# A ConvFFN down projection from seven half products, and tail norms from one product with a matrix of ones

## The chip, the cores and the metric

One NeuronCore of a Trainium2 chip runs the kernel. The metric is the device time of one execution in microseconds, as the median of the timed runs. Everything is in f32.

## The reference, cut to what matters

Two layers over 1088 tokens (1024 of a prompt, 64 of eight sampled sequences), model width 1024, hidden width 2816. Each layer mixes the tokens (a recurrence in the first, attention in the second), then runs a convolutional feed-forward net. What follows the mixer is here called the tail of a layer:

```python
x = x + rmsnorm(mo, g[1])            # mo: the mixer's output after its last matrix
hn = rmsnorm(x, g[2])
fo, cs = conv_ffn(hn, conv0[layer], ...)
x = x + rmsnorm(fo, g[3])            # layer 0: rmsnorm(x, ...) of the next layer follows

def rmsnorm(x, g):
    y = xf * lax.rsqrt(jnp.mean(xf * xf, axis=-1, keepdims=True) + NORM_EPS)
    return y * g
def conv_ffn(xn, prev, wup, cw, cb, wdown):
    hid = xn @ wup                   # 1024 -> 2 * 2816
    ...                              # a convolution of three taps along the tokens
    gate, val = jnp.split(c, 2, axis=-1)
    out = (jax.nn.gelu(gate, approximate=True) * val) @ wdown   # 2816 -> 1024
```

## The kernel before

Activations lie transposed, 128 channels on the partitions and all 1088 tokens along the free axis. `m.X`, `m.H`, `m.big` (22 tiles of 1088), `m.w`, `m.tmp` and `m.lanes` are regions of SBUF that every stage cuts up anew. Each engine has its own program, written out by hand in the order in which it runs; semaphores (`wait_ge`, `then_inc`) tie them together, and nothing reorders them. Within a tail (function `tail`, called once per layer) PE runs four stages.

1. The mixer's last matrix (`mixer`, L241): 3 token blocks of 384, 384 and 320 columns (`TB`) by 8 output tiles. A block and an output tile are a unit; its sum over the contraction tiles goes to one of six PSUM banks.
2. The up projection. For f = 0, 1 and 21 the products are plain (`expand`, L269). For f = 2 to 20 (`SEVEN`) the two output tiles, two halves of the contraction and two halves of the tokens are multiplied by seven products instead of eight (`seven`, L299): sums of quarter matrices of weights are built by Pool (`weight_sums`, L622 to L633), sums of quarters of tokens once by DVE (`token_sums`, L534 to L539), and DVE and ACT combine the products. DVE then convolves (L569, L573), ACT takes the gelu (L415), DVE multiplies with the other half (`gated`, L579) into `hid`, tile f of `m.big`.
3. The down projection (L338): again 24 units, each a sum over 22 tiles of `hid`. The weights of an output tile (1408 KB) alternate between two buffers, `wdt[0]` and `wdt[1]`, and are loaded anew for each of the three token blocks.
4. The norms, of the mixer's output with residual and following norm (p = 0), and of the down projection's output (p = 1; in the second layer without a following norm).

A norm runs block by block beside the next block's units. ACT copies the unit out of PSUM (L381) and squares it (L370), DVE adds the squares of the eight output tiles (L471). PE multiplies the sum with one column of ones, so that the tokens' sums of squares come to stand on the partitions (`statistic`, L221). ACT takes the root of three columns (L374), DVE the reciprocal of three columns (L475). PE spreads them over all partitions by a product with the identity (`spreading`, L229). DVE scales by it (L485), Pool adds the residual in `m.X` (L650), ACT squares again, and for the second norm the same follows up to L497.

The numbers count(p, n, b) say which norm of which block a semaphore has reached. SP issues all loads and stores in one queue. In the recurrence's stage (`rwkv_core`) it loads weights, a table `pv` of vectors per channel, the first key tile and eight more constants; PE, ACT and DVE each wait there for all nine loads of the semaphore `consts`. PE then builds masks with the constants (L1827, L1829) and only then computes the gates of the first pair of heads (`gates`, L1691), which ACT takes (L1337) and which DVE's scan (L1440) needs.

## Time and profile before

| | us |
|---|---|
| median of three timed runs | 4157.53 |
| lowest, highest | 4154.57, 4160.07 |
| the profiled execution, its own time | 4153.73 |
| its span | 4151.9 |

| stage of the profiled execution | from | to |
|---|---|---|
| recurrence (`rwkv_core`), first load | 402.1 | |
| first tail: mixer's last matrix | 1130.5 | 1257.8 |
| up projection | 1257.8 | 1839.7 |
| down projection | 1839.7 | 2167.2 |
| end of its norms, first load of attention | | 2189.3 |
| second tail: mixer's last matrix | 3147.2 | 3228.2 |
| up projection | 3228.2 | 3810.1 |
| down projection | 3810.1 | 4134.8 |
| end of its norms and of the last store | | 4151.9 |

Times are read from one profiled execution, in us from the start of its span; 1.8 us lie around the span. An f32 product appears as two records of PE. Records of PE's weight loads (PEld) run beside the products. A row of the timeline gives start, duration, engine, line, operation, what is written and read, and in brackets how long the engine had been idle before and who released it.

### The profile page before, as it was taken

The numbers are of one execution on the slowest core, as the hardware profiler recorded it, in microseconds if no ns is written. First come the engines' busy times: TensorE is split into PE (matmuls) and PEld (weight loads), VectorE is DVE, ScalarE is ACT, GpSimd is POOL, SyncE is SP. The second block draws the span as 40 slices with busy tenths as digits, with TensorE's granted clock in tenths as the row PEclk, the third lists the DMA queues.
The fourth block names the chain that finished last, engine by engine and source line by source line (L and its number), as shares of the span: only waits on it lengthen the run. The fifth ranks groups of instructions, "written<-read, shape, count | busy, mean of one in ns | idle before, by whom it ended". The sixth has DMA issues, their size and how long they took to land. (4 is left out here: it accounts for less than half of the span.)

```text
span 4151.9 us, 79805 instructions
## 1 busy us (share of the span) xinstructions
PE 3773.5 (91%) x35200; PEld 2817.8 (68%) x35200; DVE 1996.3 (48%) x3258; ACT 815.7 (20%) x1859; POOL 516.6 (12%) x432
## 2 busy tenths in 40 slices
PE   7998687888699999999988999999648999999998
PEld 4887566666466888865666777777535688886566
DVE  8441676666435666640124464746613566664001
ACT  6110344333121110010011222222212100001000
POOL 1221000000011222200011010101001122220001
PEclk9999899999899999999998999999768999999999
DMA  2222011010111111123321111111183111112223
GB/s 78 84 84 94 30 36 38 28 35 27 66 74 40 46 43 42 43 96 109 115 99 69 55 38 45 51 40 46 55 334 113 56 43 42 43 43 98 110 98 127
DMA packets 97216, 291.80 MB, mean 70 GB/s; under 512 B 37224, under 2 KB 52968, under 8 KB 88040
## 3 DMA queue, kind: packets, MB, share of 16 engines
q1 hardware_dynamic: 96872, 286.70, 19.5%
q8 instruction: 279, 4.57, 0.5%
q14 instruction: 65, 0.53, 0.0%
HBM read 237.71 MB, written 48.95 MB: 69 GB/s over the span
## 5 line engine op out<-in xcount | busy, mean ns | idle before, releaser
L338 PE MATMUL ps<-sb_big,sb_w 128*128 128x384 f32 (+1 forms) x2112 | 646.6, 468 | 1.2 <-ACT sb_tmp L428 1.2
L338 PEld LDWEIGHTS ps<-sb_big,sb_w 128*128 128x128 f32 x2112 | 400.2, 190 | 241.6 <-ACT sb_tmp L428 2.2
L299 PE MATMUL ps<-sb_h,sb_w 128*128 128x272 f32 x1672 | 408.1, 392 | 1.4 <-ACT sb_tmp L428 1.4
L299 PEld LDWEIGHTS ps<-sb_h,sb_w 128*128 128x128 f32 x1672 | 317.5, 190 | 67.7 <-issue 2.3
L299 PE MATMUL ps<-sb_x,sb_w 128*128 128x272 f32 x1216 | 291.1, 392 | 0.0
L471 DVE TENSOR_TENSOR sb_tmp<-sb_tmp 128x384 f32<-128x384 f32 (+1 forms) x63 | 34.8, 552 | 526.7 <-ACT sb_tmp L370 525.0
L299 PEld LDWEIGHTS ps<-sb_x,sb_w 128*128 128x128 f32 x1216 | 231.0, 190 | 47.6
L573 DVE SCALAR_TENSOR_TENSOR sb_big<-sb_tmp,sb_big 128x1024 f32<-128x1024 f32 (+1 forms) x176 | 204.0, 1159 | 13.4 <-issue 0.3
L2080 PE MATMUL ps<-sb_h,sb_w 128*128 128x384 f32 (+1 forms) x576 | 186.9, 468 | 0.0
L1099 PE MATMUL ps<-sb_x,sb_w 128*128 128x272 f32 x768 | 183.8, 392 | 0.0
L269 PE MATMUL ps<-sb_h,sb_w 128*128 128x384 f32 (+1 forms) x576 | 178.6, 470 | 3.9 <-DVE sb_tmp L548 2.1
L1099 PEld LDWEIGHTS ps<-sb_x,sb_w 128*128 128x128 f32 x768 | 145.9, 190 | 30.1
L381 ACT ACTIVATE sb_h<-ps 128x384 f32<-128x384 f32 (+1 forms) x72 | 34.0, 473 | 642.1 <-PE ps L338 598.2
L269 PEld LDWEIGHTS ps<-sb_h,sb_w 128*128 128x128 f32 x576 | 108.4, 190 | 69.3 <-issue 5.6
L2236 ACT ACTIVATE sb_w<-sb_w,sb_tmp 128x128 f32<-128x128 f32 (+1 forms) x192 | 84.9, 443 | 335.4 <-DVE sb_tmp L2341 335.4
L573 DVE SCALAR_TENSOR_TENSOR sb_w<-sb_tmp,sb_w 128x1024 f32<-128x1024 f32 (+1 forms) x176 | 142.5, 810 | 13.5 <-issue 0.4
L299 PE MATMUL ps<-sb_x,sb_lanes 128*128 128x272 f32 x608 | 145.5, 392 | 0.0
L299 PE MATMUL ps<-sb_x,sb_tmp 128*128 128x272 f32 x608 | 145.5, 392 | 0.0
L2101 PE MATMUL ps<-sb_x,sb_w 128*128 128x272 f32 x576 | 145.0, 398 | 0.0
L1773 PE MATMUL ps<-sb_tmp,sb_big 64*64 64x64 f32 x4352 | 103.0, 226 | 45.2 <-DVE sb_w L1563 32.7
L2296 DVE TENSOR_TENSOR sb_big<-sb_big,ps 128x272 f32<-128x272 f32 x120 | 52.6, 438 | 190.1 <-PE ps L2101 187.1
L1099 PE MATMUL ps<-sb_big,sb_w 128*128 128x272 f32 x576 | 140.3, 393 | 3.1 <-DVE sb_big L977 2.6
(345 smaller groups left out, 6128.0 us busy)
## 6 DMA issues: line engine op xcount, KB each, us to landing
sb_w<-wdown SPq DMA_DIRECT2D x46, 1408.0 KB, 6.0
sb_w<-wup SPq DMA_DIRECT2D x88, 512.0 KB, 4.3
sb_w<-wqkv SPq DMA_DIRECT2D x36, 512.0 KB, 3.8
sb_big<-kT SPq DMA_DIRECT2D x8, 2304.0 KB, 14.6
sb_big<-vc SPq DMA_DIRECT2D x8, 2304.0 KB, 16.3
sb_w<-wrkv SPq DMA_DIRECT2D x24, 512.0 KB, 5.4
rkv_scratch<-sb_big SPq DMA_DIRECT2D x18, 544.0 KB, 6.3
sb_big<-rkv_scratch SPq DMA_DIRECT2D x16, 544.0 KB, 3.6
```

The lines of the kernel that those rows point to most:

```text
L269: mm = pe.matmul(m.ps[:, 3 * q + b, 0:n], wt[f % 2][q][:, k, :], m.H[:, k, t0:t0 + n], start=(k == 0), stop=(k == KT - 1))
L299: mm = pe.matmul(m.ps[:, 2 * HOME[f][p] + e, 0:PIECE], w, rhs[:, k, e * PIECE:(e + 1) * PIECE], start=(k == 0 and p not in ("P2", "P3")), ...
L338: mm = pe.matmul(m.ps[:, u % 6, 0:n], wdt[u % 2][:, f, :], hid[:, f, t0:t0 + n], start=(f == 0), stop=(f == FT - 1))
L381: act.activation(out[:, k, t0:t0 + n], m.ps[:, u % 6, 0:n], ACT.Copy)
L471: dve.tensor_tensor(acc, acc, SQ[p][n][:, slot(n, b, k), 0:w], ALU.add).then_inc(summed[n], 1)
L573: ins = dve.scalar_tensor_tensor(out=out, in0=tap(j), scalar=cw(j), in1=out, op0=ALU.mult, op1=ALU.add)
L1099: mm = pe.matmul(m.ps[:, bank, 0:PIECE], lhs[:, k, :], rhs(k), start=(k == 0 and p not in ("P2", "P3")), stop=(k == 3), skip_group_check=True)
L1773: mm = pe.matmul(m.ps[o, bank, col0:col0 + C], lhs[r, c, :], rhs[r, c, :] if len(rhs.shape) == 3 else rhs[r], start=(q == 0), stop=(q == l ...
L2080: mm = pe.matmul(m.ps[:, ring(s, p), 0:w], wt[t][:, k, :], m.H[:, k, t0:t0 + w], start=(k == 0), stop=(k == KT - 1))
L2101: mm = pe.matmul(m.ps[:, ring(s, p), 0:PIECE], lhs[:, k, :], rhs[:, k, :], start=(k == 0 and n not in ("P2", "P3")), stop=(k == 3), skip_g ...
L2236: ins = act.activation(SM[n % 2][:, h, lo:2 * P], SM[n % 2][:, h, lo:2 * P], ACT.Exp, bias=nm[:, n, h:h + 1], accum_out=zz[:, n, h:h + 1])
L2296: dve.tensor_tensor(out, kept, ps, op).then_inc(ptd, 1)
```

## The change

- **Down projection.** It runs in eight pairs n of output tiles: `u = n // 4` chooses half of the tokens (544 columns, two quarters of 272), `n % 4` the pair of output tiles. The contraction is cut in two halves of 11 tiles (`HF`). Of each pair come seven products (`DOWN`, in the order P1, P7, P2, P6, P5, P4, P3), each over 11 tiles and 272 columns; P2 adds to the bank of P1 and P3 to that of P5. The four quarter matrices of weights of a pair, W11, W21, W12 and W22 (704 KB each), have one buffer each. Pool builds W3 = W11 - W21, W2 = W22 - W3, W21 = W21 + W22 and W2 = W12 - W2. DVE builds four sums of the hidden quarters (`hidden_sum`) for each half of the tokens, those of the first half for 10 of 11 rows between f = 20 and f = 21. ACT copies the products P1 and P2 out, DVE combines the other five (`combine`), and ACT squares the results.
- **Norms.** The statistic is one product of a matrix of ones with the sum of squares, so that every partition has every token's sum. ACT's root and DVE's reciprocal work on all columns (384, 320 or 272), and there is no spread. In the down projection the blocks are four quarters of 272 tokens. Blocks 0 and 1 run beside pairs 4 and 5, blocks 2 and 3 after pair 7; the second norm of these two is summed by PE, eight products each (`late_statistic`).
- **Residual.** It is loaded in two halves into other places (`XIN`) instead of in one piece into `m.X`; the results are stored in quarters.
- **Recurrence.** `pv` signals with the weights, PE computes the first gates before it waits for the constants, and DVE normalizes the first key before it waits for them.

```diff
+    HF = FT // 2
+    DOWN = ("P1", "P7", "P2", "P6", "P5", "P4", "P3")
+    BY_DVE = ("P6", "P7", "P5", "P4", "P3")
...
@@ sync
+            def part_in(n, q, r, dst, signal):
+                sp.dma_start(dst, a["wdown"][layer, 2 * (n % 4) + q, :, r * HF:(r + 1) * HF, :]).then_inc(signal, 16)
...
-            for u in range(2, NU):
-                sp.wait_ge(product, NU + u - 1)
-                sp.dma_start(wdt[u % 2], a["wdown"][layer, u % KT]).then_inc(wd[u % 2], 16)
...
+            for n in range(1, NDOWN):
+                sp.wait_ge(product, down(n - 1, "P7"))
+                part_in(n, 0, 0, W11, a11_in)
...
+                sp.wait_ge(product, down(n - 1, "P5"))
+                part_in(n, 1, 0, W21, a21_in)
+                sp.wait_ge(sums_done, WSUMS + 4 * n)
+                part_in(n, 0, 1, W12, a12_in)
+                sp.wait_ge(product, down(n - 1, "P4"))
+                part_in(n, 1, 1, W22, a22_in)
@@ tensor
-            def statistic(p, n, b):
-                pe.wait_ge(summed[n], NSUM * p + (KT - 1) * (b + 1))
-                acc = ACC[p][n][:, b % 2 if n == 0 else 0, :]
-                for j, (t0, w) in enumerate(subs(b)):
-                    mm = pe.matmul(m.ps[0:w, 6, j:j + 1], acc[:, t0:t0 + w], m.ones[:, 0:1], start=True, stop=True)
-                mm.then_inc(stat, 1)
...
+            def statistic(n, b):
+                pe.wait_ge(summed[n], (KT - 1) * (b + 1))
+                w = TB[b][1]
+                pe.matmul(m.ps[:, 6, 0:w], m.ones[:, :], ACC[n][:, b % 2 if n == 0 else 0, 0:w], start=True,
+                          stop=True).then_inc(stat, 1)
...
-                    for f in range(FT):
...
-                        mm = pe.matmul(m.ps[:, u % 6, 0:n], wdt[u % 2][:, f, :], hid[:, f, t0:t0 + n], start=(f == 0), stop=(f == FT - 1))
...
+            def seventh(n, p):
+                u = n // 4
+                lhs, rhs = {"P1": (W11, lambda k: half(u, 0, 0)[:, k, :]), "P7": (W3, lambda k: tsum(3, k, k + 1)[:, 0, :]),
+                            "P2": (W12, lambda k: half(u, 1, 0)[:, k, :]), "P6": (W2, lambda k: tsum(2, k, k + 1)[:, 0, :]),
+                            "P5": (W21, lambda k: half(u, 0, 1)[:, k, :]), "P4": (W22, lambda k: tsum(4, k, k + 1)[:, 0, :]),
+                            "P3": (W2, lambda k: half(u, 1, 1)[:, k, :])}[p]
...
+                for k in range(HF):
+                    if (n, p, k) == (0, "P7", HF - 1):
+                        pe.wait_ge(hidden, FT + 1)
+                    mm = pe.matmul(m.ps[:, BANK[n, p], 0:PIECE], lhs[:, k, :], rhs(k), start=(k == 0 and p not in ("P2", "P3")),
+                                   stop=(k == HF - 1), skip_group_check=True)
...
@@ vector
+                if f == FT - 2:
+                    for j in (3, 1, 2, 4):
+                        hidden_sum(j, 0, 0, HF - 1)
+            for j in (3, 1, 2):
+                hidden_sum(j, 0, HF - 1, HF)
+            hidden_sum(4, 0, HF - 1, HF).then_inc(hidden, 1)
...
+            def block_invert(n, b):
+                dve.wait_ge(rooted, stat_at(n, b))
+                dve.reciprocal(DROOT[b % 2], DROOT[b % 2])
...
+            block_residual(2, meanwhile=lambda: block_invert(0, 3))
+            block_residual(3)
+            dve.drain()
+            for k in range(4):
+                dve.tensor_tensor(XS[1][:, k, :], XIN[3][:, k, :], TMP2[1][:, k, :], ALU.add).then_inc(conv, 1)
+            if two_norms:
+                block_invert(1, 2)
+                block_normed(2)
+                block_invert(1, 3)
+                block_normed(3)
@@ gpsimd
+            for n in range(NDOWN):
+                pool.wait_ge(a11_in, 16 * (n + 1))
+                pool.wait_ge(a21_in, 16 * (n + 1))
...
+                pool.tensor_tensor(W3, W11, W21, ALU.subtract).then_inc(sums_done, 1)
+                pool.wait_ge(a22_in, 16 * (n + 1))
...
+                pool.tensor_tensor(W2, W22, W3, ALU.subtract).then_inc(sums_done, 1)
+                pool.tensor_tensor(W21, W21, W22, ALU.add).then_inc(sums_done, 1)
...
+                pool.wait_ge(product, down(n, "P6"))
...
+                pool.tensor_tensor(W2, W12, W2, ALU.subtract).then_inc(sums_done, 1)
@@ rwkv_core
-            sp.dma_start(pv, a["pv"].rearrange("i p n -> p i n")).then_inc(consts, 16)
+            sp.dma_start(pv, a["pv"].rearrange("i p n -> p i n")).then_inc(ld_w, 16)
...
-            pe.wait_ge(consts, 9 * 16)
+            for g in range(3):
+                gates(0, g)
+            pe.wait_ge(consts, 8 * 16)
```

The order of PE at the start of the first layer's down projection. Before, nine units of 22 products run without a break, then come the first statistic (L221) and its spread (L229):

```order
L269 MATMUL ps<-sb_h,sb_w 128x384 x16
L269 MATMUL ps<-sb_h,sb_w 128x320 x8
L338 MATMUL ps<-sb_big,sb_w 128x384 x198
L221 MATMUL ps<-sb_ones,sb_tmp 128x1 x3
L338 MATMUL ps<-sb_big,sb_w 128x384 x22
L229 MATMUL ps<-sb_ident,sb_small 128x128 x3
```

In the changed kernel (whose lines are numbered anew; L424 is `seventh`) the products of pair 0 stand there, P1, P7, P2, P6, P5, P4 (in two regions) and P3, the last one together with P1 of pair 1:

```order
L424 MATMUL ps<-sb_big,sb_w 128x272 x11
L424 MATMUL ps<-sb_x,sb_tmp 128x272 x11
L424 MATMUL ps<-sb_big,sb_w 128x272 x11
L424 MATMUL ps<-sb_x,sb_w 128x272 x11
L424 MATMUL ps<-sb_big,sb_tmp 128x272 x11
L424 MATMUL ps<-sb_x,sb_w 128x272 x10
L424 MATMUL ps<-sb_lanes,sb_w 128x272
L424 MATMUL ps<-sb_big,sb_w 128x272 x22
```

Each product needs another weight matrix, three of them made by Pool or shared with its sums. Pool had only the residual's additions there, long after the last weight sums of the up projection (L622 to L633):

```order
L632 TENSOR_TENSOR sb_w<-sb_w,sb_lanes 128x384 [waits t0_up]
L633 TENSOR_TENSOR sb_tmp<-sb_w,sb_lanes 128x128
L650 TENSOR_TENSOR sb_x<-sb_x,sb_tmp 128x384 [waits t0_scaled,x_moved]
L650 TENSOR_TENSOR sb_x<-sb_x,sb_tmp 128x384 [waits t0_scaled] x6
L650 TENSOR_TENSOR sb_x<-sb_x,sb_tmp 128x384 [waits t0_applied]
```

Now it makes four sums of 1408 columns per pair, of which each waits for a load or for a product that last read the buffer (pairs 0 and 1):

```order
L931 TENSOR_TENSOR sb_tmp<-sb_w,sb_tmp 128x1408 [waits t0_conv,t0_a21_in,t0_a11_in]
L938 TENSOR_TENSOR sb_w<-sb_w,sb_tmp 128x1408 [waits t0_hidden,t0_a22_in]
L939 TENSOR_TENSOR sb_tmp<-sb_tmp,sb_w 128x1408
L949 TENSOR_TENSOR sb_w<-sb_w 128x1408 [waits t0_product,t0_a12_in]
L931 TENSOR_TENSOR sb_tmp<-sb_w,sb_tmp 128x1408 [waits t0_product,t0_a21_in,t0_a11_in]
L938 TENSOR_TENSOR sb_w<-sb_w,sb_tmp 128x1408 [waits t0_product,t0_a22_in]
```

In pairs 4 and 5 eight residual additions stand between L939 and L949. On DVE the sums of the hidden halves (L732 to L738) have come in between the gating of f = 20 (L725) and the convolution of f = 21:

```order
L725 TENSOR_TENSOR sb_big<-sb_big,sb_w 128x1088 [waits t0_conv,t0_gelu]
L732 TENSOR_TENSOR sb_x<-sb_big 128x2720 [waits t0_hidden]
L734 TENSOR_TENSOR sb_big<-sb_big 128x10x272
L737 TENSOR_TENSOR sb_x<-sb_big 128x2720
L738 TENSOR_TENSOR sb_x<-sb_x,sb_big 128x2720
L709 COPY sb_tmp<-sb_tmp 128x2 [waits t0_padded,t0_rows_out1,t0_vec1]
```

Before, the convolution followed the gating directly.

## Rows read from the trace of the kernel before

**Rows 1.** Page: busy us (share) xinstructions; a line group, busy and mean ns.

```profile
PE 3773.5 (91%) x35200; PEld 2817.8 (68%) x35200; DVE 1996.3 (48%) x3258; ACT 815.7 (20%) x1859; POOL 516.6 (12%) x432
...
L2296 DVE TENSOR_TENSOR sb_big<-sb_big,ps 128x272 f32<-128x272 f32 x120 | 52.6, 438 | 190.1 <-PE ps L2101 187.1
```

**Rows 2.** Chain of waits, second tail: start, us, what.

```profile
3291.07 487.92 PE ps L299 x2128
...
3810.09 127.98 PE ps L338 x396
3938.07 0.56 PE ps L221 x6
...
3952.93 0.67 PE ps L229 x6
...
4134.84 0.02 issue
```

**Rows 3.** Busy us by window, engines PE, PEld, DVE, ACT, POOL; granted clock.

```profile
1321.00:1809.00 488.00, 487.60 (x2128) 403.94 (x2126) 296.66 (x494) 48.73 (x95) 111.99 (x92) 1.00 0.13 43
1840.00:2167.00 327.00, 327.00 (x1104) 205.63 (x1103) 42.12 (x77) 29.67 (x68) 15.35 (x16) 1.00 0.34 125
3147.00:3228.00 81.00, 71.20 (x240) 44.86 (x240) 37.57 (x67) 29.57 (x69) 16.59 (x16) 0.91 0.23 85
```

**Rows 4.** Timeline, first tail, last up products and start of the down projection.

```profile
1819.01 1.29 DVE L579 TENSOR_TENSOR sb_big<-sb_big,sb_w 128x1088 f32<-128x1088 f32 x1
...
1825.16 0.17 DVE L563 COPY sb_tmp<-sb_tmp 128x2 f32<-128x2 f32 x1 [4.86 <-ACT sb_tmp L428]
...
1839.71 30.58 PE L338 MATMUL ps<-sb_big,sb_w 128*128 128x384 f32 x94 [0.59 <-ACT sb_tmp L428]
...
1844.42 1.29 DVE L579 TENSOR_TENSOR sb_big<-sb_big,sb_w 128x1088 f32<-128x1088 f32 x1
```

**Rows 5.** Lines: xcount, ns min/median/max, first and last start, forms.

```profile
L622 POOL TENSOR_TENSOR sb_tmp<-sb_w x38: 1265/1267/1957, 1315.2 to 3738.8; 128x512 f32<-128x512 f32 x38
...
L2064 POOL TENSOR_TENSOR sb_w<-sb_w x12: 1254/1266/2307, 2196.9 to 2867.2; 128x512 f32<-128x512 f32 x12
...
L534 DVE TENSOR_TENSOR sb_x<-sb_h x2: 2424/2424/2425, 1296.2 to 3266.5; 128x2176 f32<-128x2176 f32 x2
...
L1542 DVE RECIPROCAL sb_lanes<-sb_lanes x8: 1845/1846/1853, 561.7 to 1117.3; 128x272 f32<-128x272 f32 x8
```

**Rows 6.** Loads: xcount, KB each, median us from issue to landing.

```profile
sb_w<-wdown SPq DMA_DIRECT2D x46, 1408.0 KB, 6.0
sb_w<-wup SPq DMA_DIRECT2D x88, 512.0 KB, 4.3
```

**Rows 7.** Timeline of PE, second tail's mixer stage.

```profile
3190.83 0.83 PE L221 MATMUL ps<-sb_ones,sb_big 128*128 128x1 f32 x6 [3.35 <-DVE sb_big L471]
3191.52 4.24 PE L241 MATMUL ps<-sb_big 128*128 128x384 f32 x8
...
3219.31 1.44 PE L221 MATMUL ps<-sb_ones,sb_big 128*128 128x1 f32 x6 [4.71 <-DVE sb_big L471]
```

**Rows 8.** Timeline, end of the first tail.

```profile
2167.16 0.44 ACT L381 ACTIVATE sb_h<-ps 128x320 f32<-128x320 f32 x1 [11.75 <-PE ps L338]
...
2185.26 3.76 DVE L497 SCALAR_TENSOR_TENSOR sb_h<-sb_x,sb_gains,ps 128x320 f32<-128x320 f32 x8 [1.93 <-PE ps L229]
2189.29 1.28 SPq L2032 DMA_DIRECT2D sb_w<-wqkv  x3
```

**Rows 9.** Timeline, end of the second tail.

```profile
4139.64 6.57 POOL L650 TENSOR_TENSOR sb_x<-sb_x,sb_tmp 128x320 f32<-128x320 f32 x8 [66.87 <-DVE sb_tmp L485]
```

**Rows 10.** Timeline, start of the recurrence.

```profile
411.50 1.55 PE L1827 MATMUL ps<-sb_tmp 64*64 64x64 f32 x24 [14.46 <-DMA sb_tmp<-c_level]
...
413.56 3.90 PE L1691 MATMUL ps<-sb_big,sb_tmp 64*64 64x384 f32 x24
...
418.51 2.42 DVE L1440 TENSOR_TENSOR_SCAN sb_big<-sb_tmp,sb_big 128x1088 f32<-128x1088 f32 x1 [3.29 <-ACT sb_big L1337]
```

More of the change, by code:

```diff
@@ L143, in tail @@
-        norms = [2, 2 if g_next is not None else 1]
-        subs = lambda b: [(j * P, min(P, TB[b][1] - j * P)) for j in range((TB[b][1] + P - 1) // P)]
-        def count(p, n, b):
-            return 2 * NBLK * p + norms[p] * b + n + 1
+        ACC = (tiles(m.big, 17 * T + 3 * BW, 2, BW), tiles(m.big, 17 * T + 7 * BW, 1, BW))
+        SQ = (tiles(m.big, 17 * T, 3, BW), tiles(m.big, 17 * T + 5 * BW, 2, BW))
+        TMP = tiles(m.big, 17 * T + 8 * BW, 3, BW)
+        W11, W12, W22, W2 = (tiles(m.w, j * HF * P, HF, P) for j in range(4))
@@ L401, in _ @@
-            collect(0)
-            root(0, 0, 2)
+                    act.wait_ge(added, KT * b + k + 1)
+                    square(1, b, k, m.X[:, k, t0:t0 + n]).then_inc(squared, 1)
+            for b in range(NBLK):
+                for k in range(KT):
+                    take(b, k)
+                    if b and k == 0:
+                        root(0, b - 1)
+                    if b and k == 2:
+                        squares(b - 1)
+                    if b and k == 5:
+                        root(1, b - 1)
@@ L404, in _ @@
+            root(0, 2)
             for s in range(4):
@@ L479, in residual @@
+            def residual(b):
                 t0, w = TB[b]
-                dve.wait_ge(spread, count(p, 0, b))
+                dve.drain()
                 for k in range(KT):
@@ L654, in rwkv_inputs @@
+            pool.wait_ge(m.x_moved, stored + 32)
+            for b in (2, 3):
+                for k in range(KT if b == 2 else 4):
+                    k += 0 if b == 2 else 4
+                    block_scaled(b, k)
+                    pool.tensor_tensor(XS[b - 2][:, k, :], XIN[b][:, k, :], TMP2[b - 2][:, k, :], ALU.add).then_inc(added, 1)
 def rwkv_inputs(m, a, scratch):
@@ L1830, in _ @@
             mm.then_inc(small_ps, 1)
-            for g in range(3):
-                gates(0, g)
             key_sums(0)
```

560 lines of the change are left out of this document (385 added, 175 removed).

## The prediction

> **What bounds the kernel now.** I read the page's busy shares first: PE works 91% of the span and no other engine more than half [rows 1]. A share is only an average, so next comes the chain of waits, stage by stage. From 3291 us on, the chain of the second layer's tail is almost nothing but PE: 487.9 us of up products, then the down stage from 3810.09 to 4134.84, broken only by the small norm products of L221 and L229 [rows 2]. The reader should see that no DMA and no other engine stands between them. The windows say the same of the first layer: in 1840 to 2167 PE is busy for 327.0 of 327.0 us at granted clock 1.00, DVE for 42, ACT for 30, Pool for 15 [rows 3]. So in the down stage columns fewer on PE are time off the end, as long as weights, sums and evictions keep up. In the second layer's mixer window (3147 to 3228) it is otherwise: the clock is 0.91 and PE waits 3.35 us and 4.71 us for DVE's additions [rows 3, 7]. There a gain on PE alone brings nothing.
>
> **The change part by part.**
>
> **Down stream, second layer.** Before: 4134.84 - 3810.09 = 324.75 us [rows 2]. After: 8 pairs of output tiles, 7 products each, 11 contraction tiles, and each f32 product stands as two PE records: 8 x 7 x 11 x 2 = 1232 records of 272 columns. The up stage has just this shape, with fewer factors per product: 487.92 us for 2128 records, 0.2293 us each [rows 2]. 1232 x 0.2293 = 282.5 us, one product 5.04 us, one pair ("cycle") 35.3 us. Three statistics stand in the stream (blocks 0, 1 and 2), two records of 272 columns each: 3 x 0.46 = 1.4. Together 283.9, a change of **-40.9**.
>
> **Down stream, first layer.** Before: from 1839.71 [rows 4] to the last eviction at 2167.16 [rows 8], 327.4 us. After: 282.5 + five statistics (2.3) = 284.8. A change of **-42.6**.
>
> Those two terms hold only with cover, so here is one cycle, counted from the start of P1: P7 ends at 10.1, P2 at 15.1, P6 at 20.2, P5 at 25.2, P4 at 30.2, P3 at 35.3.
> - Pool's sums. A sum of 512 columns takes 1.27 us, up to 2.31 when it meets other work [rows 5]. For 1408 columns that is 3.5 to 6.3 us, four per cycle 14 to 25 of 35.3 us. The tightest is W3 of the next pair: W21 is asked for at 25.2 when P5 is done. 704 KB lies between loads of 4.3 us (512 KB) and 6.0 us (1408 KB) [rows 6], so it lands at about 30 and W3 is ready at 33.5 to 37.5. P7 wants it at 40.3. W2 starts when P3 ends and is ready 3.5 to 6.3 later for P6 at 50.4, W21+W22 by 42 to 48 for P5 at 55.4, the last one starts at 20.2 for P3 at 30.2. None is late; the least slack is 2.8 us. In pairs 4 and 5 Pool has eight residual additions of under 1 us between its third and fourth sum; it starts them at 7 to 13 and is through by 20 or so. I take no stall.
> - SP issues four weight loads per cycle; behind its waits for products only the next weight loads and the residual's transfers are queued, and W11, W12 and W22 have over 10 us of slack.
> - DVE combines five products (an addition of a PSUM tile of 272 columns takes 0.44 us [rows 1]) and adds squares. In pair 3 four sums of the hidden halves come on top. The same kind of subtraction takes 2.42 us for 2176 columns [rows 5], so 3.3 for 2992: 13.3 us in a cycle where it else has little to do. Six PSUM banks let PE run about five products ahead. In pairs 4 and 5 DVE's norm work ends near 24, and the statistic that waits for it stands at 25.2: 1 to 2 us of slack, the second tightest place.
>
> **Start of the down stage.** P7 of pair 0 needs the hidden sums. 40 of 44 rows are added after the tile f=20 is gated (L579 at 1819.01 plus 1.3): four instructions of 2720 columns at 3.0, 12.1 us, until 1832.4. DVE was idle 4.86 us before 1825.16 and then until 1839.7; the convolution of f=21's first half moves to about 1837 [rows 4]. W3 is then ready at 1841 to 1843.5, while P1 keeps PE until 1844.75. The last tile is gated at 1845.7 and four small sums end at about 1847.6; P7 reaches that tile at 1849.3. All hidden, cost 0; if the sums took twice as long, the second convolution would be late and up to 10 us would show in each layer.
>
> **Norms of the mixers.** From L221 to L229 14.86 us pass, where a unit alone takes 127.98 / 9 = 14.22: 0.64 for a statistic, and 0.67 for a spread, 1.31 us for the two [rows 2]. One product with ones of 384 columns costs 0.65, of 320 columns 0.54. First layer, all PE-bound: 4 x 0.66 + 2 x 0.77 = **-4.1**. On DVE the reciprocal grows: 1.85 us for 272 columns [rows 5], so 2.6 for 384, where before it worked on three columns. In the first layer this replaces the wait of one PE unit for the spread. In the second layer DVE's chain bounds: the residual steps start about as before (reciprocal against spread), so I count 0 in the stream (between -2.5 and +3) and **-1.5** for the two norms that fall into the first up products.
>
> **Tail of each layer.** Before, second layer: 17.1 us from 4134.84 to the end of the span. After, from the end of P3: combine, square, add 1.5; eight scalings in 0.42 to 0.47 steps (3.76 us for eight of 320 columns [rows 8]) with a reciprocal of 1.85 in the middle until 6.9; eight more until 10.3; four additions on DVE until 11.8; the last quarter's store about 5. That is 17: **0** (-1 to +2). The old chain had Pool in step with DVE, 6.57 us of additions from 4139.64 [rows 9]; the new one has more on DVE and less handshake. First layer: 22.1 us from 2167.16 to the next stage's first load at 2189.29 [rows 8]. After: squares of the last block by 14.3, sums on PE 15, and on DVE reciprocal, 3.4, reciprocal, 3.4: 22.7. **+0.6** (-1 to +4).
>
> **Start of the recurrence.** PE waited until 411.50 for the last constants, ran the masks and only then the gates at 413.56; ACT took them and DVE's scan began at 418.51 [rows 10]. With the gates ahead of the constants they run from about 405, the masks at 411.5 stay, and the scan can begin at about 414.5, after the masks: **-4.0** (-1.5 to -5). Everything behind it hangs on this chain.
>
> **Sum.** -40.9 - 42.6 - 4.1 - 1.5 + 0 + 0.6 - 4.0 = -92.5. On the profiled execution's own 4153.73 us: 4061.2. The median of the three runs is 3.8 above it, so as a median 4157.53 - 92.5 = **4065**.
>
> **A rule weighed against a row.** Pool's sum of L2064 takes 1.27 us in the median and 2.31 at worst, while DVE subtracts SBUF tiles beside it [rows 5]. The Trainium skill (SBUF - State Buffer, Who interferes with whom) says that a DVE instruction with two SBUF inputs and a GpSimd instruction that reads SBUF exclude each other for their whole length. By the rule every such meeting costs the later one the rest of the earlier; the trace agrees with it in that row. It would put each sum near the upper figure in pair 3 and change nothing elsewhere, since the combines of the steady cycle read PSUM.
>
> **The rivals.**
> - *Supply.* The W3 sum misses P7. For: it is the tightest handover, its load is issued 15 us before it is wanted, W12's load follows it closely, and a 1408-column sum was never seen. Against: with both upper prices 2.8 us remain. If load and sum together took 17 us instead of 15.1, 2 us would be lost in 14 handovers: +28, **4093**.
> - *Ends.* The work without cover costs more: reciprocals and DVE additions against Pool's at the two ends, hidden sums at the two starts, DVE in the second mixer. 3 us in each of four places: +12, **4077**. For: most rows there are scaled from other widths. Against: none is far.
> - *Slower than before: the clock.* In the second mixer PE waits 3.35 us, and the eight records after it take 4.24 us [rows 7], where 8 x 0.323 = 2.6 is full pace [rows 2]: 1.6 more; after the last such wait the small statistic takes 1.44 instead of 0.83. If P7 waited so in each cycle, the low level (1.2 GHz) would cost as much again as the time spent at it. To be slower than before, 92.5 us must be lost in 14 handovers, 6.6 us each: a wait of 5 us and 1.6 for the clock. It decides when load and sum take 20 us instead of 9. The result, with 7 us each, is 14 x 7 = +98, **4163 or more**. Against: the up stage cycles banks in the same way at granted 1.00 [rows 3]. The Trainium skill (TensorE: Matmul & The Clock Gate, A second HAM failure mode: psum-queue depth-cycling) tells of a kernel whose clock swung because PE cycled PSUM banks with short gaps; rows 3 speak against it here.
> - *The norms and the recurrence bring nothing* (the part that would not do what it says): 4.1 + 1.5 + 4.0, **4075**. For: PE's own saving is worth something only where PE bounds, and in the second mixer it does not; at the recurrence DVE might wait for the masks rather than for the gates. Against: in the first mixer PE is the bound, and the gates of rows 10 stand plainly between masks and scan.
>
> **How the numbers follow.** Forecast within about 8 us of 4065: 0.66. Ends or norms, 4073 to 4082: 0.18. Supply, 4080 to 4100: 0.10. More gain than forecast (DVE's chain in the second mixer shortened by 2.5, more at the recurrence), down to 4052: 0.03. Slower: 0.02. The rest is no change: 0.01. The range that leaves out no more than two in ten goes from 4050 to 4086. What a measurement here can tell from no change is about 0.2%, 8 us. Faster by more: 0.97; within: 0.01; slower: 0.02.
>
> **What would show it.** Right: each down stage one PE block of about 284 us at clock 1.00, with no wait of P7 or of the statistic of pair 4; product after product every 5.04 us; the scan of the recurrence at about 414.5; DVE's reciprocals of 2.6 us. Wrong: Pool's 1408-column sums above 6.3 us, idle time of PE before P7 released by Pool, a granted clock under 1.00 inside the stage, or more than 19 us after the last product.

## The result, and the profile after

The changed kernel takes 4101.25 us (median of four runs, 4098.92 to 4110.88) beside 4156.05 for the kernel before in the same comparison: a ratio of 0.9872, 95% interval 0.9853 to 0.9892. A second comparison gave 4105.65 and 0.9862 (0.9844 to 0.988). It is faster, by 55 us instead of the 92.5 that were forecast, and lies outside the range of 4050 to 4086. The profiled execution took 4103.14 us, its span is 4101.4.

The page's shares, columns as in [rows 1]:

```profile
PE 3695.6 (90%) x35376; PEld 2868.7 (70%) x35376; DVE 2264.6 (55%) x3406; ACT 821.6 (20%) x1870; POOL 738.8 (18%) x504
```

PE is still busy 90% of the span. The windows over the two down stages show a little more, where [rows 3] had idle-free stretches at clock 1.00 (columns: stretch, its length, busy time and count of PE, PEld, DVE, ACT, Pool, granted clock, DMA share, GB/s):

```profile
1844.20:2142.40 298.20, 288.98 (x1242) 237.57 (x1242) 128.64 (x135) 29.07 (x70) 114.38 (x48) 0.99 0.28 93
3786.80:4079.50 292.70, 286.42 (x1238) 235.87 (x1238) 112.94 (x103) 21.97 (x52) 114.29 (x48) 0.99 0.28 95
```

PE idles 9.2 us in the first and 6.3 in the second. The first stage is 13.4 us longer than the forecast 284.8, so another 4.2 us are not idle: records of PE that take longer than the forecast pace, where the granted clock is under 1.00. Two windows of 7 us, one behind the longest wait and one behind a wait of 2.92 us, columns as above:

```profile
1858.20:1865.20 7.00, 6.96 (x23) 5.57 (x24) 0.00 (x0) 0.00 (x0) 0.00 (x0) 0.76 0.31 103
2023.40:2030.40 7.00, 6.99 (x24) 5.62 (x25) 3.17 (x4) 0.81 (x2) 3.16 (x1) 0.79 0.32 133
```

PE is busy there without a gap, but part of the time at the lower of its two clock levels (1.2 instead of 2.4 GHz): 23 and 24 records stand where the forecast pace would put 30 or 31. Elsewhere the chain runs at the forecast pace (columns: start, length, what):

```profile
3800.81 128.43 PE ps L424 x552
...
3947.95 127.88 PE ps L424 x558
```

The waits of PE in the first down stage, summed by releaser (columns: sum in us, times, longest):

```profile
PE ps L424 <- DVE sb_lanes L738: 4.2, 1, 4.2
PE ps L393 <- DVE sb_tmp L787: 2.9, 1, 2.9
PE ps L393 <- DVE sb_tmp L781: 1.5, 1, 1.5
PE ps L424 <- issue: 0.6, 1, 0.6
PE ps L424 <- DVE sb_h L834: 0.6, 1, 0.6
```

Four of the five are VectorE's, none is the weights', and none is a wait for Pool's sums. The largest stands at the start of the stage, at the last contraction tile of P7. Its surroundings in time (columns: start, length, engine, line, operation, tiles, count, idle time before and what ended it):

```profile
1849.28 1.29 DVE L725 TENSOR_TENSOR sb_big<-sb_big,sb_w 128x1088 f32<-128x1088 f32 x1
...
1850.60 0.44 DVE L732 TENSOR_TENSOR sb_x<-sb_big 128x272 f32<-128x272 f32 x1
1850.79 3.27 POOL L938 TENSOR_TENSOR sb_w<-sb_w,sb_tmp 128x1408 f32<-128x1408 f32 x1 [6.10 <-DVE sb_big L725]
1850.96 3.40 DVE L734 TENSOR_TENSOR sb_big<-sb_big 128x272 f32<-128x272 f32 x1
1854.02 3.34 POOL L939 TENSOR_TENSOR sb_tmp<-sb_tmp,sb_w 128x1408 f32<-128x1408 f32 x1
1854.43 3.23 DVE L737 TENSOR_TENSOR sb_x<-sb_big 128x272 f32<-128x272 f32 x1
1857.74 0.44 DVE L738 TENSOR_TENSOR sb_lanes<-sb_x,sb_big 128x272 f32<-128x272 f32 x1
...
1858.24 0.72 PE L424 MATMUL ps<-sb_x,sb_tmp 128*128 128x272 f32 x2 [4.15 <-DVE sb_lanes L738]
```

The gating of the last row (L725) releases Pool's sum W2 (L938) and VectorE's four small hidden sums at the same moment. Two of the four take 0.44 us. The two that meet a sum of Pool take 3.40 and 3.23 us: each ends 0.3 us after a sum of Pool does. The rule of the Trainium skill that the prediction weighed (SBUF - State Buffer, Who interferes with whom) describes this: a VectorE instruction with two SBUF inputs and a GpSimd instruction that reads SBUF exclude each other for their whole length. The trace agrees with it here.

The other place is the norms. The scalings with the root (L636; kernel before L485) read their factor from `m.lanes` now and read it from PSUM before:

```profile
3151.62 8.77 DVE L636 SCALAR_TENSOR_TENSOR sb_big<-sb_h,sb_gains,sb_lanes 128x384 f32<-128x384 f32 x8
```

Eight of them take 8.77 us; in the kernel before, the eight between 3178.09 and 3184.26 took 6.17. At the end of the program, where [rows 9] show 6.57 us of Pool's additions, VectorE and Pool now alternate in the same way:

```profile
4081.13 2.74 DVE L804 SCALAR_TENSOR_TENSOR sb_w<-sb_big,sb_gains 128x272 f32<-128x272 f32 x4
4081.78 3.43 POOL L955 TENSOR_TENSOR sb_x<-sb_big,sb_w 128x272 f32<-128x272 f32 x4 [14.48 <-DVE sb_w L804]
...
4085.56 7.95 DVE L804 SCALAR_TENSOR_TENSOR sb_w<-sb_big,sb_gains 128x272 f32<-128x272 f32 x12
4086.03 3.69 POOL L955 TENSOR_TENSOR sb_x<-sb_big,sb_w 128x272 f32<-128x272 f32 x4 [0.83 <-DVE sb_w L804]
```

Twelve scalings take 7.95 us, 0.66 each, where I had counted 0.42 to 0.47. It is not the factor's place by itself: near the end of the first tail, where Pool has nothing to do, eight scalings that also read their factor from SBUF take 3.39 us, 0.42 each:

```profile
2160.81 3.39 DVE L820 SCALAR_TENSOR_TENSOR sb_h<-sb_x,sb_gains,sb_big 128x272 f32<-128x272 f32 x8
```

Stage by stage, each kernel in two profiles. The stages run from the first product of one to the first product of the next, the recurrence from its first scan on VectorE:

| stage | before | after | forecast | measured |
|---|---|---|---|---|
| up to the first scan | 418.5, 420.8 | 415.2, 414.7 | -4.0 | -3.3 to -6.1 |
| recurrence | 712.0, 717.6 | 725.0, 715.5 | 0 | scatter |
| first mixer and up stage | 709.2, 709.2 | 704.1, 704.3 | -4.1 | -5.0 |
| first down stage and tail | 355.1, 355.6 | 331.0, 329.7 | -42.0 | -25.0 |
| attention | 952.4, 951.5 | 943.3, 947.6 | 0 | scatter |
| second mixer | 81.0, 84.4 | 88.7, 89.2 | 0 | +6.2 |
| second up stage | 581.9, 581.9 | 579.6, 579.6 | -1.5 | -2.3 |
| second down stage to the end | 341.8, 341.6 | 314.6, 315.8 | -40.9 | -26.5 |

Leaving the two rows of scatter out, -57 is measured where -92.5 was forecast. Most of the 37 us between forecast and median lie in three rows: 17 in the first down stage and tail, 14 in the second, 6 in the second mixer. The other three rows came out 2 us better than forecast.

### The profile page after: what moved, and what is told of

Its sections match the earlier page's. It is cut to its first block and busy times, and to the rows that moved or that the text cites. A ratio compares the mean times of both kernels' runs of the same rounds, so it can differ in the third digit from the quotient of the medians.

```text
span 4101.4 us, 80718 instructions
## 1 busy us (share of the span) xinstructions
PE 3695.6 (90%) x35376; PEld 2868.7 (70%) x35376; DVE 2264.6 (55%) x3406; ACT 821.6 (20%) x1870; POOL 738.8 (18%) x504
## 5 line engine op out<-in xcount | busy, mean ns | idle before, releaser
L367 PE MATMUL ps<-sb_x,sb_w 128*128 128x272 f32 x1216 | 291.1, 392 | 0.0
L367 PEld LDWEIGHTS ps<-sb_x,sb_w 128*128 128x128 f32 x1216 | 231.0, 190 | 47.6
L424 PE MATMUL ps<-sb_big,sb_w 128*128 128x272 f32 x1056 | 251.4, 396 | 2.5 <-issue 1.3
L424 PEld LDWEIGHTS ps<-sb_big,sb_w 128*128 128x128 f32 x1056 | 202.6, 192 | 46.5 <-issue 4.3
L1403 PE MATMUL ps<-sb_x,sb_w 128*128 128x272 f32 x768 | 183.8, 392 | 0.0
L1403 PEld LDWEIGHTS ps<-sb_x,sb_w 128*128 128x128 f32 x768 | 145.9, 190 | 30.1
L424 PE MATMUL ps<-sb_x,sb_w 128*128 128x272 f32 x672 | 160.1, 394 | 0.0
L746 DVE TENSOR_TENSOR sb_big<-sb_big,ps 128x544 f32<-128x544 f32 x38 | 27.4, 721 | 233.5 <-PE ps L367 233.4
L424 PEld LDWEIGHTS ps<-sb_x,sb_w 128*128 128x128 f32 x672 | 128.4, 191 | 26.8
L2406 PE MATMUL ps<-sb_x,sb_w 128*128 128x272 f32 x576 | 145.0, 398 | 0.0
```

The costliest lines, as they stand in the source:

```text
L367: mm = pe.matmul(m.ps[:, 2 * HOME[f][p] + e, 0:PIECE], w, rhs[:, k, e * PIECE:(e + 1) * PIECE], start=(k == 0 and p not in ("P2", "P3")), ...
L424: mm = pe.matmul(m.ps[:, BANK[n, p], 0:PIECE], lhs[:, k, :], rhs(k), start=(k == 0 and p not in ("P2", "P3")), stop=(k == HF - 1), skip_gr ...
L746: dve.tensor_tensor(U2, U2, pair_ps(f, "P6"), ALU.add).then_inc(parted, 1)
L1403: mm = pe.matmul(m.ps[:, bank, 0:PIECE], lhs[:, k, :], rhs(k), start=(k == 0 and p not in ("P2", "P3")), stop=(k == 3), skip_group_check=True)
L2406: mm = pe.matmul(m.ps[:, ring(s, p), 0:PIECE], lhs[:, k, :], rhs[:, k, :], start=(k == 0 and n not in ("P2", "P3")), stop=(k == 3), skip_g ...
```

## The experiments

**Two theories on the 37 us.** *Exclusion*: VectorE's instructions with two SBUF inputs wait for Pool's and the other way round, at the start of each down stage, in the norms and in the tails. *Rivals*: the small sums are slow by themselves, the long reciprocal (2.55 us against 0.18) is what makes the second mixer late, the statistics simply stand too early, and the reordered recurrence costs the 13 us by which it was longer in the first profile.

**The recurrence alone, and everything but the recurrence.** The first kernel is the one before with this part of the change alone, the second the changed kernel without it:

```diff
-            pe.wait_ge(consts, 9 * 16)
+            for g in range(3):
+                gates(0, g)
+            pe.wait_ge(consts, 8 * 16)
...
-            for g in range(3):
-                gates(0, g)
```

> The kernel before with one part of the change alone: the recurrence's gates and first key ahead of the wait for the constants. In the changed kernel the first scan starts 3.3 us earlier (415.18 against 418.51), yet the recurrence ends 10.0 us later (1135.1 against 1125.1). Theory A, the reordering itself does it (it shifts the phase of PE against DVE from pair to pair): the recurrence ends at about 1135 here too and the time is 4156 + 10 = 4166. Theory B, something that the rest of the change brings into this stage does it (nothing else in this stage was edited, but all later code has other lengths): the recurrence ends near 1121.8 and the time is 4156 - 3.3 = 4153.

> The changed kernel with the recurrence put back as it was before. Theory A (the reordering costs 13 us inside the recurrence): its end moves from 1135.1 back to 1125.1, time 4101 - 10 = 4091. Theory B (the rest of the change does it): the end stays 13 us late, so about 1138, time 4101 + 3 = 4104.

The reordering alone gave 4153.72 beside 4158.23: ratio 0.999 (0.998 to 0.9999), so -4 us, with the first scan at 415.1. Without it the changed kernel took 4102.14, ratio 0.9862 (0.9844 to 0.9879), no difference that can be told from 0.9872 or 0.9862. From first scan to mixer they show 720.9 and 717.5 us. Theory A predicted +10 for the first and falls: the reordering is worth about the 4 us forecast.

**The changed kernel and the one before, unedited.**

> The changed kernel once more, without an edit. Its first profile shows 725.0 us from the first scan of the recurrence to the mixer's first product, the kernel before 712.0, and two edited kernels whose recurrence is the same code as here show 719.6 and 712.9. If the recurrence's length varies from one execution to the next, this profile shows another figure between 710 and 727 with every other stage within 1 us of the first profile (up stages 579.6, second down stage 292.7). Rival, the 13 us belong to the program: 725 again. Median time 4096 to 4106 either way.

> The kernel before once more, without an edit. Its first profile shows 712.0 us from the first scan of the recurrence to the mixer's first product and 81.0 us for the second mixer; the kernel with its recurrence reordered, but the same mixer, showed 84.1 for the latter. If the first profile was a short execution of both stages, this one gives 714 to 724 and 82 to 85. Rival: 712 and 81 again, and then the rest of the change has lengthened both by some microseconds.

The same program's recurrence took 715.5 us instead of 725.0. The windows from the first to the last scan (seven pairs of heads) in the two executions of the changed kernel, columns as for the down stages:

```profile
415.20:959.60 544.40, 423.88 (x15513) 340.38 (x15513) 364.05 (x597) 202.88 (x393) 30.81 (x26) 0.94 0.10 32
```

```profile
414.70:949.10 534.40, 414.71 (x15513) 336.98 (x15509) 364.24 (x598) 202.61 (x393) 30.83 (x26) 0.96 0.11 32
```

Seven pairs took 544.4 us in the one and 534.4 in the other. So the 13 us by which the first two profiles differ are scatter of this stage; in the fifteen profiles of this case it spans 707 to 725 us. The kernel before, again, shows 717.6 for it and 84.4 for the second mixer, so its first profile had a short execution of both. The up stages and the down stages of the kernel before repeat to 0.1 us. I had expected the same of the changed kernel, within 1 us, and that was wrong: its down stages took 296.7 and 294.0 us this time instead of 298.2 and 292.7, with the same waits of PE. The clock is what differs in the first: behind the wait of 2.93 us it was 1.00 this time, where the first profile had 0.79.

```profile
2013.50:2020.50 7.00, 6.99 (x31) 5.82 (x32) 3.72 (x6) 1.24 (x3) 3.16 (x1) 1.00 0.39 143
```

In the recurrence the two windows show the same number of PE's records and the same busy time of VectorE, but PE is busy 9.2 us longer in the longer one, at a granted clock of 0.94 against 0.96. So the clock goes with most of this difference. It is not the whole rule of the stage (the shortest of the fifteen, 707 us, had 0.95 in this stretch), and what lowers it in one execution and not in the next stays open.

**Small hidden sums ahead of Pool's.**

```diff
                 if n == 0:
-                    pool.wait_ge(hidden, FT)
+                    pool.wait_ge(hidden, FT + 1)
```

> The changed kernel, with GpSimd's second and third weight sum of pair 0 held until the four sums of the last hidden row are done. Theory: a VectorE instruction with two SBUF inputs and a GpSimd instruction wait for one another; two subtractions of 272 columns took 3.40 and 3.23 us instead of 0.44 because they met GpSimd's sums of 3.3 us, and the product behind them waited 4.15 us and ran 1.85 us slow afterwards. Then all four take 0.44 here, the wait before 1858.24 is gone, and each layer gains 6.0: 4101 - 12 = 4089. Rival, the subtractions are slow by themselves there (first touch of the row, a semaphore): they stay at 3.2 to 3.4 us and the time at 4101 or, since GpSimd starts later, up to 4105.

4083.05 us, ratio 0.9822 (0.9803 to 0.984). The same stretch as above, VectorE and Pool:

```profile
1846.31 0.44 DVE L732 TENSOR_TENSOR sb_x<-sb_big 128x272 f32<-128x272 f32 x1
1846.67 0.43 DVE L734 TENSOR_TENSOR sb_big<-sb_big 128x272 f32<-128x272 f32 x1
1847.17 0.44 DVE L737 TENSOR_TENSOR sb_x<-sb_big 128x272 f32<-128x272 f32 x1
1847.69 0.44 DVE L738 TENSOR_TENSOR sb_lanes<-sb_x,sb_big 128x272 f32<-128x272 f32 x1
1848.35 3.16 POOL L938 TENSOR_TENSOR sb_w<-sb_w,sb_tmp 128x1408 f32<-128x1408 f32 x1 [7.95 <-DVE sb_lanes L738]
...
1851.47 3.16 POOL L939 TENSOR_TENSOR sb_tmp<-sb_tmp,sb_w 128x1408 f32<-128x1408 f32 x1
```

All four take 0.44 us, Pool's sums 3.16 instead of 3.27 and 3.34, and PE goes on without a gap. The first down stage falls from 298.2 to 292.4 us, the second from 292.7 to 286.6. The expected 12 us are in the stages; the median fell by more, since its runs scatter by 14 us. The rival (slow by themselves) is out.

**Root and reciprocal in PSUM.** For the mixers the edit is the first pair of lines, for the tails the second, with the late statistics of the first layer in PSUM banks of their own:

```diff
-        ROOT = m.lanes[:, 0:BW]
+        ROOT = m.ps[:, 7, 0:BW]
...
-        DROOT = [hid[:, 2 * KT + c, 0:PIECE] for c in range(2)]
+        AT = lambda n, b: m.ps[:, b - 2 if (n, b) in ((1, 2), (1, 3)) else 6 + b % 2, 0:PIECE]
```

> The changed kernel with root and reciprocal written to PSUM instead of SBUF, in the mixers and in the tails. The scalings then read one SBUF tile and one PSUM tile, as in the kernel before. Theory (VectorE with two SBUF inputs and GpSimd exclude each other): the second mixer's eight scalings between 3151.62 and 3160.39 took 8.77 us where the kernel before took 6.17 in the same place; here they take 6.2, two such blocks lie on the second mixer's path: -5, the second tail loses the contention of about 5 us, the first tail 5, time 4101 - 13 = 4088. Rival, the longer reciprocal alone (2.55 us against 0.18) makes the second mixer late: the scalings stay at 8.8 us, and the time at 4101.

> The changed kernel with the factor of the mixers' norms alone in PSUM, that of the tails left in SBUF. Theory (exclusion of VectorE with two SBUF inputs and GpSimd): the second mixer stage falls from 89 (88.7 to 91.5 in five profiles) to about 85, the eight scalings from 8.8 to 6.2 us, while the down stages, the first tail (33 to 35 from the last down product to the next stage's first product) and the second (21.8) stay: 4101 - 5 = 4096. Rival: most of the 20 us that both places gave together came from somewhere else: the stage stays at 89.

Both places gave 4083.04, ratio 0.9822 (0.9807 to 0.9838); the mixers alone 4095.94, ratio 0.9846 (0.9829 to 0.9863). By stages the first is 13 to 14 us shorter than the two profiles of the changed kernel, as expected; the rest of its gain is scatter. The mixers' scalings in the changed kernel and in the one with the factor in PSUM (columns: count, shortest, median and longest in ns, first and last start in us):

```profile
L636 DVE SCALAR_TENSOR_TENSOR sb_big<-sb_h,sb_gains,sb_lanes x24: 545/1246/1356, 3151.6 to 3222.3; 128x384 f32<-128x384 f32 x16, 128x320 f32<-128x320 f32 x8
```

```profile
L636 DVE SCALAR_TENSOR_TENSOR sb_big<-sb_h,sb_gains,ps x24: 540/610/616, 3138.8 to 3203.1; 128x384 f32<-128x384 f32 x16, 128x320 f32<-128x320 f32 x8
```

Operation, size and work are the same; only the place of one operand differs, and the median goes from 1.246 to 0.610 us. The reciprocal is as long in PSUM (2.57 us) as in SBUF (2.55). The second mixer took 84.6 and 84.5 us, against 88.7 to 91.5 in the kernels with the factor in SBUF; PE's waits for the sums ahead of its statistics fell from 18.1 to 13.0 us. The kernel before took 84.4 us there, 84.1 with the reordered recurrence and 81.0 in its first profile, so whether 1 or 2 us are still lost cannot be told. At the end of the program:

```profile
4063.45 1.72 DVE L804 SCALAR_TENSOR_TENSOR sb_w<-sb_big,sb_gains,ps 128x272 f32<-128x272 f32 x4
...
4066.86 5.08 DVE L804 SCALAR_TENSOR_TENSOR sb_w<-sb_big,sb_gains,ps 128x272 f32<-128x272 f32 x12
```

Twelve scalings now take 5.08 us instead of 7.95, and from the last product to the end 18.2 us pass instead of 21.9. With the mixers alone the end stays at 21.9. The theory of exclusion holds in size and place.

**The reciprocal, by the old form of the second layer's mixer norms.** On top of the three edits, this kernel takes the statistic as a column, the reciprocal of three columns and the spread by PE, in that place alone:

```diff
+                if by_column:
+                    dve.reciprocal(RINV[n], RCOL[n]).then_inc(inverted, 1)
+                    return
                 dve.reciprocal(ROOT[:, 0:TB[b][1]], ROOT[:, 0:TB[b][1]])
```

> As the kernel with all three edits, but the second layer's mixer norms in their old form (sums as a column, reciprocal of three columns, spread by PE into PSUM). In that stage VectorE's chain is the bound and the reciprocal of 384 columns takes 2.55 us against 0.18. If the reciprocal is on the path, the stage from the second mixer's first product to the first up product goes from 84.6 to about 80, and the time is 4 us less than with all three edits. Rival: the two PE operations and the handshakes of the old form cost as much as the reciprocal (stage 84, time the same), as I predicted for the changed kernel.

4077.77, ratio 0.9798 (0.978 to 0.9816), against 0.979 with the new form; the stage takes 85.6 us against 85.2. The rival of this run is what happened: a reciprocal of 2.57 us costs no more there than a spread with its two handshakes. So it is not what made the second mixer late. The two norms that fall into the first up products do cost more in the old form: the up stage behind takes 582.0 us instead of 579.6.

**Statistics later, alone and with the other two.**

```diff
-                    if (n, p) == (4, "P7"):
+                    if (n, p) == (4, "P2"):
...
-                    if n in (4, 5) and p == "P5" and two_norms:
+                    if n in (4, 5) and p == "P4" and two_norms:
```

> The changed kernel with the statistic of block 1 behind the third product of pair 4 instead of the second, and the statistics of the second norm behind the sixth product instead of the fifth. In the first profile PE waits 1.50 and 2.92 us for them in the first layer and 1.50 in the second, and runs slow behind each. If they wait only because they stand too early, the waits go and the first down stage gets 5 us shorter (298.2 to 293), the second 2 (292.7 to 291): 4101 - 7 = 4094. Rival: the work behind them (VectorE's chain of norms in pairs 4 and 5) gets late by the same amount and stops PE at the next statistic or combination: 4101.

> The changed kernel with all three edits: small hidden sums ahead of GpSimd's, root and reciprocal in PSUM, late statistics. The gains measured apart (about 18, 20 by ratio) and expected (7) lie at different places, so if the causes are independent they add up: 4101 - 15 - 18 - 7 = 4061, down stages of 286 and 285, which is about what was predicted for the changed kernel. Rival, two of them remove the same wait in pairs 4 and 5 (the scalings are shorter already): 4070.

> The changed kernel with small hidden sums first and root and reciprocal in PSUM, statistics where they were. If the late statistics brought nothing but another wait (alone they moved the time by 0 in the comparison with the kernel before, 0.986 against 0.987 and 0.986), the down stages are 287 to 289 here and the time within 3 us of all three edits. Rival: with the other two causes away the statistics' place is worth its 5 us in the first layer: 291 here against 286.2.

Alone: 4103.92, ratio 0.986 (0.9841 to 0.9879), no gain that the time can show. The stage does show one: the first down stage takes 293.4 us instead of 298.2 and 296.7, the second 292.5 instead of 292.7 and 294.0. The waits of 1.50 and 2.92 us are gone, but PE now waits behind the late statistic for ScalarE:

```profile
1999.57 3.68 PE L424 MATMUL ps<-sb_big,sb_w 128*128 128x272 f32 x15 [1.34 <-ACT sb_big L586]
```

All three edits: 4073.02, ratio 0.979 (0.9767 to 0.9812), 12 us above the sum that I expected. The two without the late statistics: 4072.46, ratio 0.9787 (0.9771 to 0.9802). The down stages of the two kernels, the two edits first (columns as for the down stages above):

```profile
1840.30:2129.60 289.30, 285.62 (x1242) 235.53 (x1242) 117.83 (x135) 28.83 (x70) 112.35 (x48) 1.00 0.29 96
3768.00:4054.60 286.60, 284.44 (x1238) 234.85 (x1238) 101.91 (x103) 21.91 (x52) 112.23 (x48) 1.00 0.29 97
```

```profile
1845.90:2133.30 287.40, 285.36 (x1242) 235.80 (x1242) 119.75 (x135) 29.08 (x70) 111.94 (x48) 1.00 0.29 97
3777.80:4064.20 286.40, 284.43 (x1238) 234.99 (x1238) 101.68 (x103) 21.93 (x52) 112.15 (x48) 1.00 0.29 97
```

The expectations put 286.2 us on record for both stages of the second kernel; the trace gives 287.3 and 286.4. So the statistics' place is worth 2.0 us in the first layer beside the other two edits, 3 to 5 us without them, and 0.2 us in the second layer. The times cannot show it, since recurrence and attention scatter by more. With the factor in PSUM the wait of 2.92 us has become 1.53, because the scalings ahead of it are shorter, and so less is left for the later place to gain.

**Who holds up pair 4.** The wait that only changed its name I first put down to ScalarE standing at the root of block 1:

```diff
                 if n == 4:
                     block_root(0, 0)
-                    block_root(0, 1)
...
+                if n == 4:
+                    block_root(0, 1)
```

> The kernel with all three edits, and ScalarE's root of block 1 in pair 4 moved behind its eviction of the third product. With the late statistic ScalarE stood at that root and kept the bank of the first product, so PE waited 1.33 to 1.35 us in each layer for ScalarE instead of the 1.50 for VectorE. If that is the whole cause, both waits and the slow products behind them go: each down stage 286.2 to about 284.5, which is the predicted 284.8 and 283.9, and the time is 3 us less than with all three edits, ratio to the kernel before about 0.978. Rival: VectorE's chain of pair 4 is what is late, and the wait turns up at the next statistic (stages stay at 286).

That was wrong. The stages stayed at 287.3 and 286.4 and the wait at 1.33 and 1.34. (The time of 4066.69, ratio 0.9773, 0.9758 to 0.9787, is lower by what recurrence and attention scatter.) VectorE's rows of that kernel lead further back:

```profile
3905.07 5.78 DVE L739 TENSOR_TENSOR sb_x<-sb_x,sb_big 128x2720 f32<-128x2720 f32 x1
3910.92 0.44 DVE L739 TENSOR_TENSOR sb_lanes<-sb_x,sb_big 128x272 f32<-128x272 f32 x1
3911.46 0.44 DVE L835 TENSOR_TENSOR sb_h<-sb_h,ps 128x272 f32<-128x272 f32 x1
```

The last hidden sum of pair 3 takes 5.78 us beside Pool's sum, where it takes 2.99 alone, and the combination of P3, whose products ended at about 3900.7, comes only at 3911.46 (10.8 us late, more than the 5.8 that I wrote ahead of the last run). ScalarE squares its result before it evicts the P1 of pair 4, and so PE waits with P2. The last run has the three edits, without the move of ScalarE's root, and puts that sum behind the combination:

```diff
-                if n == 3:
-                    hidden_sum(4, 1, 0, HF - 1)
-                    hidden_sum(4, 1, HF - 1, HF).then_inc(hidden, 1)
...
                 combine(n, "P3")
                 block_add(n, 3)
+                if n == 3:
+                    hidden_sum(4, 1, 0, HF - 1)
+                    hidden_sum(4, 1, HF - 1, HF).then_inc(hidden, 1)
```

> The kernel with small hidden sums first, factors in PSUM, the second norm's statistics behind the sixth product, and in pair 3 the fourth hidden sum behind the combination and the square of the last product instead of before them. In its old place this sum of 2720 columns took 5.78 us beside GpSimd's sum (3.0 alone), and the combination behind it came 5.8 us after its product; from there the wait at the statistic (1.5 us) or, with the statistic later, at ScalarE's eviction (1.33). If this sum is the cause, the combination starts at once, PE no longer waits in the first 15 us of pair 4, and each down stage goes from 286.2 to about 284.8 (first) and 284.5 (second); ratio to the kernel before 0.977. Rival: the chain of norms behind it, now later by the sum, stops PE within pair 4 (stages 286 or more).

```profile
3901.72 0.44 DVE L834 TENSOR_TENSOR sb_h<-sb_h,ps 128x272 f32<-128x272 f32 x1
3902.72 2.23 DVE L781 TENSOR_TENSOR sb_tmp<-sb_tmp 128x272 f32<-128x272 f32 x1 [0.56 <-ACT sb_tmp L557]
3905.04 2.99 DVE L738 TENSOR_TENSOR sb_x<-sb_x,sb_big 128x2720 f32<-128x2720 f32 x1
```

The sum takes 2.99 us, since Pool is through by then, and the wait is gone. What the meeting costs has moved to the addition before it (L781, 2.23 instead of 0.44), where nobody waits. The two down stages in windows:

```profile
1826.90:2112.60 285.70, 285.07 (x1242) 236.16 (x1242) 118.70 (x135) 29.22 (x70) 111.81 (x48) 1.00 0.28 97
3755.30:4040.10 284.80, 284.17 (x1238) 235.39 (x1238) 101.64 (x103) 22.09 (x52) 111.95 (x48) 1.00 0.29 98
```

The clock is 1.00, idle time 0.6 us in each, and 285.7 and 284.8 us compare with the forecast 284.8 and 283.9. The time is 4068.43, ratio 0.9776 (0.9762 to 0.9789). Together with the kernel before it in this list (0.9773) it is the fastest here, about 1% under the changed kernel and about 92 us under the kernel before. That is the gain that I had forecast for the change itself, but by a few us it is luck: the stages outside recurrence and attention show 89 us, the rest is their scatter.

## Why the prediction was right or wrong

- **What bounds it: right.** PE columns saved are time saved. The 1232 records are there, and away from the waits they take the forecast 0.2293 us: in the second down stage's chain 552 records take 0.2327 us each, with the slow start behind the first wait, and the later 558 take 0.2292. The weights came in time: no wait of PE names a load or a Pool sum.
- **Down stream: the rate right, the two stages 13 and 9 us too short** (298.2 and 292.7 against 284.8 and 283.9). The steps that failed are named below; with them mended the runs gave 285.7 and 284.8. In the first stage 9.2 us of the 13 are waits of PE and 4 are slow records behind them. Of the signs of being wrong that I had named, a granted clock under 1.00 inside the stage (0.99) and more than 19 us after the last product (21.9) came true, the two on Pool's sums did not.
- **Start of the down stage, "all hidden, cost 0": the step that failed first.** I let the four small sums end at 1847.6, 1.9 us after gating, at their length alone. Pool's W2 and W21 sums start at the same release, and the four took 7.6 us. PE waited 4.15 us, and the 24 records behind the wait took 7.3 us instead of 5.5, at a granted clock of 0.76: about 6 us in each layer, undone by the edit that holds Pool back (5.8 and 6.1). I had priced such a slow start (1.6 us) in the rival on the clock, but only for waits on Pool. I had weighed the rule of exclusion and applied it to Pool's sums of pair 3 alone ("would change nothing elsewhere"), since I asked which large operations meet. What it cost was the small ones: a meeting costs the rest of the longer partner, whatever the length of one's own.
- **DVE's slack in pairs 4 and 5: right that this place is tight, wrong that it holds.** Statistic of block 1 late by 1.50, that of the second norm by 2.92 in pair 4. The causes were a hidden sum of 5.78 us where I had 3.3, and scalings slowed by Pool. With the factor in PSUM the 2.92 became 1.53, and in the last run, which also has the later statistics, both waits are gone.
- **Pool's large sums: right.** Mean 3.17 to 3.36 us against 3.5 to 6.3. The rival Supply had a chance of 0.10 and did not occur.
- **Norms of the mixers: first layer right (-5.0 against -4.1, where my terms add up to 4.2), second layer wrong (+6.2 against 0).** I compared reciprocal with spread, and that comparison was right: the old form in that place took as long (85.6 against 85.2). The step left out is that the factor moved from PSUM to SBUF, which gives each scaling a second SBUF input beside Pool's additions: 1.246 us instead of 0.610. Undoing it gave back 4 of the 6 us.
- **Tails: wrong by 5 us each** (27.9 us from the last product to attention's first load against 22.7, 21.9 to the end against 17). The cause is the same: 0.42 to 0.47 us per scaling came from [rows 8], whose scalings read PSUM. It was a price from a row with another operand, and it holds for SBUF only where Pool is idle. With the factor in PSUM the two take 23.9 and 18.2; the 1.2 us that are left in each are not explained.
- **Start of the recurrence: right.** -3.3 at the first scan, -4 us in time for this part alone.
- **The rivals.** "Ends" named the right places and the right sort of cause, with 12 us where 37 were lost, and had 0.18 together with the norms. Its terms of 3 us each were guesses on widths, and the meetings of VectorE and Pool that filled them were not worked out. The forecast of faster (0.97) was right.

## What to carry to other kernels

When a change gives GpSimd longer instructions, list every VectorE instruction with two SBUF inputs that can run beside them, the short ones first, and price each meeting at the rest of GpSimd's instruction. Keep a factor that many VectorE operations read in PSUM, if GpSimd works beside them. And price an operation from a row with the same operands in the same memories, not only the same shape.

## What the runs showed of the hardware

A VectorE subtraction of 272 columns takes 0.44 us alone and 3.23 to 3.40 beside a GpSimd sum of 3.3 us; one of 2720 columns 2.99 and 5.78. One SBUF operand moved to PSUM halves a scaling of 384 columns beside GpSimd's additions (median 1.246 to 0.610 us), while a reciprocal of 384 columns takes 2.55 us in SBUF and 2.57 in PSUM. Eight scalings of 272 columns with the factor in SBUF take 3.39 us while GpSimd is idle, 0.42 each, as with the factor in PSUM.

Behind a wait of TensorE of 4.15 us the granted clock was 0.76 in the 7 us read here; behind one of 2.92 us it was 0.79 in one execution, and 1.00 in the next behind one of 2.93. So a wait can cost 1.5 to 1.8 us more than its length, and not each time.

A program on one core scatters by stage: the up stages repeat to 0.1 us, the down stages of the changed kernel, which have waits, to 1.5, and a recurrence of many small dependent products spans 707 to 725 us over executions. So one pair of profiles can show a difference of 13 us that the change has not made.
